# One diffusion layer on 8 cores: K and Q weights issued in another order, and attention's modulations summed on DVE

## What is computed

```python
def hybrid_layer(x, ctx, mod_lat, mod_ctx, g1, w_in, q_g, k_g, w_f, w_out, g2, w1, w2, tabs, update_ctx):
    sh1, sc1, gt1, sh2, sc2, gt2 = jnp.split(mod_lat, N_MOD, axis=-1)
    ...
    hc = modulate(rmsnorm(ctx, g1), csh1, csc1)          # context: K and V only
    ...
    h = modulate(rmsnorm(x, g1), sh1, sc1)
    q, k, v, u = split_proj(h @ w_in)                    # 12 | 4 | 4 heads of 128, 512 Fourier channels
    q = apply_axial_rope(rmsnorm(heads(q, N_Q_HEADS), q_g), tabs)
    k = apply_axial_rope(rmsnorm(heads(k, N_KV_HEADS), k_g), tabs)
    attn = latent_attention(q, k, v, kc, vc)             # softmax over context and latent keys
    four = fourier_mix(u, w_f)
    x = x + gt1 * (jnp.concatenate([attn, four], axis=-1) @ w_out)
    h2 = modulate(rmsnorm(x, g2), sh2, sc2)
    x = x + gt2 * sq_relu_mlp(h2, w1, w2)
```

## Time and profile before

| | |
|---|---|
| median of 3 runs | 1749.67 us (lowest 1747.08) |
| the profiled execution | 1748.87 us |
| its slowest core (7), first to last instruction | 1747.3 us |
| spans of the eight cores | 1736.9 to 1747.3 us |
| PE busy | 1579.0 us, 90% |
| DVE / ACT / POOL busy | 718.5 / 570.3 / 420.5 us |
| attention, 436 to 706 us: PE / ACT / DVE busy | 262.47 / 225.69 / 78.15 us |

### The profile page before, as it was taken

One profiled execution on the slowest core, in us unless ns is written; L12 is line 12 of the kernel. 1 busy time (PEld: TensorE's weight loads), 2 busy tenths in 40 slices (PEclk: granted clock), 3 DMA queues, 4 the chain that ended last, 5 costly groups with the idle time before them and its releaser, 6 DMA issues.

```text
span 1747.3 us, 28023 instructions; the slowest of 8 cores (1736.9 to 1747.3 us)
## 1 busy us (share of the span) xinstructions
PE 1579.0 (90%) x9252; PEld 788.6 (45%) x9252; DVE 718.5 (41%) x1134; ACT 570.3 (33%) x946; POOL 420.5 (24%) x238
## 2 busy tenths in 40 slices
PE   0179789698999999998899999999999999999996
PEld 0045334344666666444444444444444444444443
DVE  0057667477233222364233333333333333333226
ACT  1046145233888888104511111111111111111133
POOL 1000025243100010040033133431334214342230
PEclk9999999899999999999999999999999999999998
DMA  7999947484983979553632654446453563536614
GB/s 143 172 257 252 165 74 120 86 122 70 170 146 71 148 138 153 159 83 49 97 49 49 97 74 72 69 78 97 66 80 59 87 97 56 88 51 96 114 35 165
DMA packets 90685, 185.82 MB, mean 106 GB/s; under 512 B 3888, under 2 KB 63024, under 8 KB 86832
## 3 DMA queue, kind: packets, MB, share of 16 engines
q0 software_dynamic: 78640, 142.65, 53.1%
q1 hardware_dynamic: 11904, 41.39, 7.1%
HBM read 318.28 MB, written 8.39 MB: 187 GB/s over the span
## 4 chain that ended last, share of the span: by engine, by line
PE 73%; DMA 12%; DVE 7%; issue 3%; ACT 2%; POOL 1%; DVEq 0%; POOLq 0%; SPq 0%; ACTq 0%
PE psum L283 71%; DMA arena<-w_ada 9%; DVE arena L290 3%; DMA arena<-qkg 2%; DVE arena L638 1%; PE psum L287 1%; DMA arena<-x_own 1%; DMA arena<-w 1%; ACT arena L391 1%; DVE arena L296 1%; POOL arena L290 1%; DVE arena L431 1%; ACT arena L640 0%; DVE arena L981 0%; ACT arena L642 0%
## 5 line engine op out<-in xcount | busy, mean ns | idle before, releaser
L283 PE MATMUL psum<-arena 128*128 128x512 bf16 (+5 forms) x8572 | 1542.4, 348 | 131.1 <-DMA arena<-w_ada 73.5
L283 PEld LDWEIGHTS psum<-arena 128*128 128x128 bf16 (+3 forms) x8572 | 745.1, 99 | 898.7 <-issue 191.1
L290 DVE TENSOR_TENSOR arena<-psum,arena 128x512 f32<-128x512 f32 (+2 forms) x602 | 408.5, 715 | 633.3 <-PE psum L283 590.5
L290 POOL TENSOR_TENSOR arena<-arena 128x2048 bf16<-128x2048 bf16 (+1 forms) x104 | 312.0, 3014 | 355.8 <-DMA arena<-w 247.4
L1084 ACT ACTIVATE arena<-psum 128x512 f32<-128x512 f32 x128 | 75.3, 588 | 656.7 <-PE psum L283 656.7
L841 ACT ACTIVATE arena<-psum 128x768 bf16<-128x768 f32 x288 | 226.5, 810 | 43.8 <-PE psum L283 36.6
L280 POOL DMA_DIRECT2D arena<-w_ada x48 | 36.1, 752 | 392.3 <-PE psum L283 361.6
L290 DVE TENSOR_TENSOR arena<-arena 128x256 f32<-128x256 f32 (+3 forms) x163 | 104.4, 640 | 28.4 <-ACT arena L1151 10.8
L391 ACT ACTIVATE arena<-arena 128x2048 bf16<-128x2048 f32 x26 | 49.6, 1908 | 190.0 <-DVE arena L290 108.1
L280 POOL DMA_DIRECT2D arena<-w x24 | 25.4, 1057 | 296.6 <-PE psum L283 253.1
L1086 ACT ACTIVATE arena<-arena 128x512 bf16<-128x512 f32 x128 | 80.6, 629 | 12.1 <-ACT arena L1084 0.4
(11 more groups left out here) (44 smaller groups left out, 262.4 us busy)
## 6 DMA issues: line engine op xcount, KB each, us to landing
arena<-w_ada POOLq DMA_DIRECT2D x48, 1024.0 KB, 13.9
arena<-w POOLq DMA_DIRECT2D x24, 2048.0 KB, 17.1
arena<-x_own SPq DMA_DIRECT2D x16, 1024.0 KB, 17.0
arena<-w_in POOLq DMA_DIRECT2D x7, 2048.0 KB, 21.8
arena<-w POOLq DMA_DIRECT2D x8, 1536.0 KB, 13.6
arena<-x_oth SPq DMA_DIRECT2D x8, 1024.0 KB, 12.3
out<-arena SPq DMA_DIRECT2D x16, 512.0 KB, 2.8
arena<-w_out POOLq DMA_DIRECT2D x3, 2048.0 KB, 19.0
```

The source lines that it names most:

```text
L283: S.add('pe', lambda e, o_=out, l=lhsT, r=rhs, a=start, b=stop, kw=kw: e.matmul(o_, lhsT=l, rhs=r, start=a, stop=b, **kw), reads=reads, wr ...
L290: S.add(eng, lambda e, o_=out, a=in0, b=in1, op=op: e.tensor_tensor(out=o_, in0=a, in1=b, op=op), reads=reads, writes=writes)
```

## The change

Two things are changed.

First, the order of the early transfers. The K weights (block 3) are no longer issued right behind the V projections, but behind the first `next(g_sh)` of c = 0, which issues the last piece (p = 7) of m = 0. The Q weights (block 0) are issued in the K stage's unit t = 1 instead of t = 9. And `shift_rows` with the first two groups of `shift` stands ahead of the last `project_v`, the third group behind the `SHB` product.

Second, m = 2, 3 and 5 are summed on DVE. For each of 16 row groups, two `scalar_tensor_tensor` operations of 128 by 1024 (L814 of the changed kernel) multiply the bf16 piece by the group's column of `silu(c)` (the new `SF`, f32) and add it to an f32 accumulator in the place of the result (`GT1` or `GT2`). At the end f32 matmuls with ones add up the 128 partitions: for m = 2 and 5 four of 512 columns, each followed by a copy on DVE; for m = 3 sixteen with the accumulator's 128 by 128 block as the weights and 2 columns. The bias of m = 2 and 5 is now one row, fetched by SP into partition 0 after DVE has zeroed the accumulator; DVE's first sum waits for it. The steps are 116 in the loop, taken from k = 12 on; a modulation step no longer shuts out a flip or a Fourier matmul, and a flip comes at `pr` = 3 instead of 2.

```diff
         v_evac(NT - 1)
-        wslot[3] = load_wb(w_in[:, 3 * 512:4 * 512])
...
             if c < 3:
                 next(g_sh)
+                if c == 0:
+                    wslot[3] = load_wb(w_in[:, 3 * 512:4 * 512])
                 next(g_sh)
...
                 for _ in g_sh:
                     pass
+                S.alias('shb', ['ada2'])
+                S.alias('ext', ['ada2'])
+                shift_rows(modcol[:, 0, :, 0:1], 'modcol0')
+                for g0, g1 in ((0, 2), (2, 4)):
+                    for kc in range(16):
+                        shift('act' if kc % 3 == 1 else 'dve', kc, g0, g1)
             bank = project_v(m_)
...
-            if t == 9:
+            if t == 1:
                 wslot[0] = load_wb(w_in[:, 0:512])
...
+        def ada_cols(m, p0, acc):
+            hk = ['gt%dh%d' % (m, h) for h in range(2)]
+            if m != 3:
+                for k in hk:
+                    S.alias(k, ['gt%d' % m])
+                S.add('dve', lambda e: e.memset(acc, 0.0), writes=['gt%d' % m])
+                dma('sp', acc[0:1, :], bgate_d[0:1, 0 if m == 2 else 1, :], 'gt%d' % m, writes=['gt%d' % m])
+                yield
+            for kc in range(16):
+                pi, a = p0 + kc // 2, kc % 2
+                i = pi % 4
+                for h in range(2):
+                    hs = slice(h * 1024, (h + 1) * 1024)
...
+                        S.add('dve', lambda e, hs=hs, i=i, a=a, kc=kc: e.scalar_tensor_tensor(out=acc[:, hs], in0=ADA2[i][:, a, hs], scalar=SF[:, kc:kc + 1], in1=acc[:, hs],
+                                                                                              op0=ALU.mult, op1=ALU.add), reads=rk, writes=[hk[h]])
+                    if h == 0 and a == 0 and kc > 0:
+                        refill()
+                    yield
+            refill()
+            if m == 3:
+                for q in range(4):
+                    for i in range(4):
+                        kc = q * 4 + i
+                        mm(PS(7)[:, kc * 2:kc * 2 + 2], acc[:, kc * 128:(kc + 1) * 128], ONESF[:, 0:2], True, True, [hk[kc // 8], 'onesf'], ['ps7'])
+                    yield
...
+            else:
+                for jb in range(4):
+                    js = slice(jb * 512, (jb + 1) * 512)
+                    mm(PS(7), ONESF, acc[:, js], True, True, [hk[jb // 2], 'onesf'], ['ps7'])
+                    yield
+                    copy('dve', acc[:, js], PS(7), ['ps7'], ['gt%d_%d' % (m, jb)])
+                    yield
...
-        NADA = 73
+        NADA = 116
...
-            if pr == 2 and ui > 0:
+            if pr == 3 and ui > 0:
                 flips.append(ui - 1)
-            if k >= 16 and (k - 15) * NADA // (len(steps) - 16) > (k - 16) * NADA // (len(steps) - 16):
+            if k >= 12 and (k - 11) * NADA // (len(steps) - 14) > (k - 12) * NADA // (len(steps) - 14):
                 next(g_ada, None)
-            elif flips and four_st[0] != 'open':
+            if flips and four_st[0] != 'open':
```

More of the change, by code:

```diff
@@ L231, in build_program @@
         dcol = AV(o, 64); o += 64
+        SF = AV(o, 64); o += 64
         assert o <= 6.5 * KB
@@ L329, in build_program @@
               reads=['ccol'], writes=['sT'])
+        S.add('act', lambda e: e.activation(out=SF, in_=ccol_t.rearrange("p (k r) -> p k r", r=2)[:, :, 0], func=AF.Silu), reads=['ccol'], writes=['sF'])
         S.add('dve', lambda e: e.memset(V1[:, :, :, 128:129], 1.0), writes=['V%d' % c for c in range(18)])
@@ L540, in build_program @@
                 copy('dve', UFX, PS(bank)[0:1, :], [pk], ['ufx'])
-        S.alias('shb', ['ada2'])
-        S.alias('ext', ['ada2'])
-        shift_rows(modcol[:, 0, :, 0:1], 'modcol0')
         for i in range(16):
             mm(PS(6), SHB[:, i, :], wbv(wslot[5])[:, i, :], i == 0, i == 15, ['shb', 'wb%d' % wslot[5]], ['ps6'])
-        for g0, g1 in ((0, 2), (2, 4), (4, 8)):
-            for kc in range(16):
-                shift('act' if kc % 3 == 1 else 'dve', kc, g0, g1)
+        for kc in range(16):
+            shift('act' if kc % 3 == 1 else 'dve', kc, 4, 8)
         for c in range(4):
@@ L772, in build_program @@
         GT2 = AV(T0 + 12 * KB, 8 * KB)
-        for k in (['mixT_%d' % t for t in range(8)] + ['on0', 'on1', 'wcs', 'alt']
+        for k in (['mixT_%d' % t for t in range(8)] + ['on0', 'on1', 'wcs', 'alt', 'onesf']
                   + ['pt%d' % i for i in range(4)] + ['abt%d_%d' % (i, j) for i in range(2) for j in range(2)]):
@@ L789, in build_program @@
         TBANK = 6
+        def ada_cols(m, p0, acc):
[6 more added lines that the diff above has]
+                yield
+            for kc in range(16):
+                pi, a = p0 + kc // 2, kc % 2
+                i = pi % 4
+                for h in range(2):
+                    hs = slice(h * 1024, (h + 1) * 1024)
+                    rk = ['adb%d' % i, 'sF'] + (['gt%d' % m] if m != 3 else [])
+                    if m == 3 and kc == 0:
+                        S.add('dve', lambda e, hs=hs, i=i, a=a, kc=kc: e.tensor_scalar(out=acc[:, hs], in0=ADA2[i][:, a, hs], scalar1=SF[:, kc:kc + 1], scalar2=None, op0=ALU.mult),
+                              reads=rk, writes=[hk[h]])
+                    else:
[11 more added lines that the diff above has]
+                    yield
+                tt('dve', modcol[:, m], PS(7)[:, 0:32].rearrange("p (j r) -> p j r", r=2), bcol[:, m].unsqueeze(2).to_broadcast([128, 16, 2]), ALU.add,
+                   ['ps7', 'bcol'], ['modcol%d' % m])
+                yield
+                S.alias('gt5', hk)
+            else:
+                for jb in range(4):
[3 more added lines that the diff above has]
+                    copy('dve', acc[:, js], PS(7), ['ps7'], ['gt%d_%d' % (m, jb)])
+                    yield
@@ L791, in ada_rest @@
+        S.add('dve', lambda e: e.memset(ONESF, 1.0), writes=['onesf'])
         def ada_rest():
-            for m in ADAORD:
-                yield from ada_gen(m, ADA2, 'adb', 7, MODROW2, SELR, {2: GT1, 5: GT2}.get(m), refill)
+            for n, m in enumerate(ADAORD):
+                yield from ada_cols(m, n * 8, GT1 if m == 2 else GT2)
         def fourier():
@@ L901, in build_program @@
                 v_bias(k // 4)
[L902 to L903 removed]
+            if k == 10:
+                for kk in ['gt2', 'gt3h0', 'gt3h1', 'gt5'] + ['gt%d_%d' % (m, j) for m in (2, 5) for j in range(4)]:
                     S.alias(kk, late)
[L905 to L908 removed]
+            if pr == 3 and ui > 0:
                 flips.append(ui - 1)
[L910 removed]
+            if k >= 12 and (k - 11) * NADA // (len(steps) - 14) > (k - 12) * NADA // (len(steps) - 14):
                 next(g_ada, None)
[L912 removed]
+            if flips and four_st[0] != 'open':
                 flip_O(flips.pop(0))
@@ L1048, in build_program @@
             if cb == 0:
-                OLDH = (['pt%d' % i for i in range(4)] + ['on0', 'on1', 'wcs', 'alt', 'selr', 'ft', 'wof0', 'wof1', 'modrow', 'ccm', 'scm', 'wfm']
+                OLDH = (['pt%d' % i for i in range(4)] + ['on0', 'on1', 'wcs', 'alt', 'onesf', 'selr', 'ft', 'wof0', 'wof1', 'modrow', 'ccm', 'scm', 'wfm']
                         + ['abt%d_%d' % (i, j) for i in range(2) for j in range(2)])
@@ L1062, in build_program @@
         for j in range(4):
-            S.alias('a2t0_%d' % j, ['wfm', 'modrow', 'selr', 'alt'])
-            S.alias('a2t1_%d' % j, ['gt2'] + ['gt2_%d' % i for i in range(4)])
+            S.alias('a2t0_%d' % j, ['wfm', 'modrow', 'selr', 'alt', 'onesf'])
+            S.alias('a2t1_%d' % j, ['gt2', 'gt2h0', 'gt2h1'] + ['gt2_%d' % i for i in range(4)])
         am_i = [0]
```

7 lines of the change are left out of this document (1 added, 6 removed).

## The result

The changed kernel takes 0.9896 of the time before, 95% interval 0.9874 to 0.9919: 18 us less (14 to 22) of 1749, some 1730 us. Executions in which cores of a die were held at a lower clock are left out of every comparison here. The forecast was 1714, the range 1703 to 1731: the time lies at its upper edge, where the rivals "DVE runs late" (1729) and "the wait only moves" (1730) had put it.

A forecast was written before the change was run, and what follows sets the result against it. PE was taken as nearly full except for early waits; in attention ACT bounds plain steps, PE those with Fourier or column-group matmuls. 1748.87 - 34.5 - 0.4 = 1714.0 us, range 1703 to 1731.

The forecast's parts named there:

- DVE runs late: Rival, attention: bias rows take 8 us or more, or lag spans the Fourier part; loses 15, time 1729; chance 0.22.
- the wait only moves: Rival, K stage: Q weights delay piece 3 onward as long as piece 6 before; time 1730; chance 0.12.
- Part 1: Early stages: the new order of transfers and shift saves 34.5 us, between 31 and 37.
- the term of 19.1 us: Before the K stage: two PE waits and slow clock go, so the `SHB` product starts 19.1 us earlier.
- Part 2: Attention: modulations m = 2, 3 and 5 summed on DVE net -0.4 us, from about -12 to +17.
- Bias rows: Attention: DVE's first sums wait for two fetched rows, 3.5 us each; +3 us for both, bounds 0 and 17.
- Closing copies: Attention's Fourier part: copies behind norms and sums on DVE make PE wait for `ps6`; +9 us, bounds 3 and 16.
- Tail: End of attention: last copy, f32 matmul and copy of m = 5 come after the last flip; +2 us.
- column groups: Attention: 48 steps with four column-group matmuls removed, 0.30 us each; -14.4 us.
- m = 3: Attention: sixteen small f32 matmuls, four in each of four steps, lengthen three steps by some 0.7; +2 us.
- flips: Attention: the Fourier part ends near k = 160, so 7 flips less stand behind a closing copy; -2 us.

The follow-up runs named there:

- k_old: Changed kernel with the K weights fetched ahead of the Fourier projections again; 0.9975 of the time before the change.
- q_late: Changed kernel with the Q weights fetched at t = 9 again; 0.9990 of the time before the change.
- shift_old: Changed kernel with `shift_rows` and all of `shift` behind the last `project_v` again; 0.9971 of the time before (0.9929 to 1.0014).
- combo_small: Changed kernel with three empty steps after each bias-row fetch, two alternating banks, all 125 modulation steps inside the loop, 16-column sums; 0.9740 of the time before.
- sums_twice: Changed kernel with each DVE sum issued twice in a row; 1838.3 us in one execution.
- bias_early: Changed kernel with three empty steps between each bias row's fetch and the first sum; 0.9837 of the time before the change.
- sums_small: Changed kernel with each sum over 16 columns instead of 1024, one bank kept; 0.9828 of the time before the change.
- row4: Changed kernel with each bias row fetched as four rows of 512 columns into partitions 0 to 3; 1736.7 us in one execution.

## Why the prediction came out as it did

**Part 1, the queue: right, with one price left out.** p = 7 ahead of the K weights removed the wait (k_old), the early Q weights removed the long one in the K stage (q_late) and put a smaller one on piece 3, 1.2 to 4.4 us over the cores where 3.6 was forecast. The K stage became 89.0 - 74.8 = 14.2 us shorter, forecast 15.4. On five cores it now takes 73.6 us, 15.3 less on average; on cores 3, 4 and 7, whose waits are the longest (3.52, 4.38 and 3.19), it takes 77.1, 78.1 and 75.7. There the matmuls behind the wait are slower, as this row of core 3 shows, where 20 matmuls otherwise take 3.96:

```profile
265.68 6.65 PE L284 MATMUL psum<-arena 128*32 128x512 bf16 x20 [3.52 <-DMA arena<-w_ada]
```

On core 4 PE was granted 0.50 of its clock from 266.45 to 269.90, the 1.2 GHz level. The forecast counted the slow clock behind the long wait that went (2.64) and put that behind its own new wait at nothing.

**Part 1, the shift: the term of 19.1 us was too large.** `shift_rows` comes 17.9 earlier (18.7 on core 7, from which the forecast was made), but the first reduction of the K stage starts only 15.4 earlier. The failed step is "the first K unit's chain on DVE starts no earlier than its third group of shifts, as before, and I take the same distance to PE". That distance grew by 2.4: `project_v`'s two operations (L545, 1.40) now stand inside it, and one shift runs against POOL (below). PE's waits for POOL's additions, 2.4 us on every core, are the same delay seen from PE: in shift_old they are at most 1.0.

**Part 2, the prices: right.** A sum takes 1.276 us, the upper figure of 1.2 to 1.28. Where these sums come one behind another nothing is lost (combo_small), and at double the price PE waits some 100 us for DVE (sums_twice).

**Part 2, the waits: three terms mis-sized.** Against -0.4 stand +8.5 in attention and +2.8 behind it.

- *Bias rows*, "+3 for both": 11.4 (bias_early), the largest miss. The row took 4.7 and 5.7 us on core 4 instead of 3.5. By the forecast's own rule, one us lost for each above 2, that is 6.4; the other 5 were lost because DVE stayed behind for several steps: in sums_small, where it has little to catch up on, 5.2 us are gone behind the second row. By the rule of the Trainium skill that the prediction weighed there (DMA: Bandwidth & Descriptors, Queues, rings and completion order) the term would have been near 0; this row, with the traffic at 1.03, measured otherwise, and what held it up is open (row4). The forecast's bound of 17 held it.
- *Closing copies*, "+9": the late closes that it counted are there at the size that it gave them. It had seven, 10 us; the trace has seven waits of over 1 us, 10.0 to 10.4, and the two behind copies of m = 2 are 1.23 and 1.02 for its 1.2. Put at nothing were the other closes: 18 short waits, 4.3 us. Together PE waits 14.3 us in this part on average, 11.5 more than before. Two banks take away more, 14.7, since waits of before end with them.
- *Tail*, "+2": 2.8 by the table; 4.0 were to be had by taking it away.

These three were too low by 8.4, 2.5 and 0.8, together the 11.7 us by which part 2 missed. What is left of the measured 8.5 + 2.8 behind 11.4, 11.5 and 2.8 is -14.4, as the forecast has it for column groups, m = 3 and flips together. That is a remainder, and none of the three was tried by itself. One reading there is loose: 0.88 instead of 0.77 would lose 0.11 us a step, and the trace's 1.10 loses 0.33, three times as much, not twice.

So the sum was off by 4.5 us in part 1 (30.0 for 34.5) and by 11.7 in part 2, both in one direction. The rival "DVE runs late" named the place, with +15 for attention. That the time fell on its 1729 is in part luck: its rows of 8 us or more did not come (4.7 to 6.4), and part 1 gave 4.5 of the 16 us. "The wait only moves" gave nearly the same time and is refuted by the K stage, 14.2 us shorter, and by q_late: two cases with one time are told apart only by stages.

## What to carry to other kernels

When work moves from a full engine to an idle one, its own time can be free (117 us for 0.6 here) and still cost through order: whatever stands ahead of a copy that frees a bank, or of a norm that a transpose waits for, is paid by the engine that waits. Before putting such work in, look which instructions of the receiving engine others wait for, give their targets a second buffer, and issue any fetch that it waits for several steps ahead. And time a change's halves apart: here one half hid 12 us that the other had lost.
